# A softmax transpose moved off TensorE: 32x32 block transposes on VectorE and SBUF-to-SBUF DMAs

## The reference

```python
def chunked_rel_attention(q, k, v, rel_bias):      # 8 heads of width 64, 512 tokens
    ...
    scores = jnp.einsum("bnqhd,bnkhd->bnhqk", qc, kb) * (dh ** -0.5)
    bias = rel_bias[:, jnp.clip(dist, -REL_CLIP, REL_CLIP) + REL_CLIP]
    scores = jnp.where(valid, scores + bias[None, None], NEG_INF)
    p = jax.nn.softmax(scores, axis=-1)
    out = jnp.einsum("bnhqk,bnkhd->bnqhd", p, vb)

def hybrid_layer(x, ...):
    hn = rms_norm_2(x, norm_gain)
    proj = hn @ w_in                               # 4096 columns
    ...                                            # ya: attention, yr: retention, 4 heads of 128
    y = jnp.concatenate([ya * silu(ag), yr * silu(rg)], axis=-1)
    return x + y @ w_out
```

## Time and profile before

| | us |
|---|---|
| time, median of 3 runs (1222.36 to 1224.81) | 1222.63 |
| the profiled execution | 1224.13 |
| its span, first to last instruction | 1222.3 |
| PE busy | 1208.9 (99%) |
| PEld busy | 1027.0 (84%) |
| DVE busy | 842.9 (69%) |
| ACT busy | 589.4 (48%) |
| POOL busy | 287.8 (24%) |

### The profile page before, as it was taken

How to read it: one execution, slowest core, us unless ns; L and a number is a source line. 1 busy time by engine, 2 the same in 40 slices (tenths; PEclk the granted TensorE clock), 3 DMA queues, 4 the chain that set the end, 5 groups by cost and what they waited for, 6 DMA issues and landing times.

```text
span 1222.3 us, 15898 instructions
## 1 busy us (share of the span) xinstructions
PE 1208.9 (99%) x6061; PEld 1027.0 (84%) x6061; DVE 842.9 (69%) x1361; ACT 589.4 (48%) x1080; POOL 287.8 (24%) x299
## 2 busy tenths in 40 slices
PE   8999999999999999999999999999999999999998
PEld 7788888888888888888888879899888889899886
DVE  5889655556776577537758887767747686766746
ACT  6666432333433334224336477664435577654442
POOL 0220499912000000000006761111414211212300
PEclk8999999999999999999999999999999999999999
DMA  7422333233423433233324332222214332222211
GB/s 218 124 83 64 101 87 103 88 102 95 130 78 90 126 96 94 86 108 100 103 70 131 90 99 88 79 85 71 69 52 138 109 91 87 78 69 71 77 45 69
DMA packets 196032, 114.35 MB, mean 94 GB/s; under 512 B 3994, under 2 KB 190836, under 8 KB 195828
## 3 DMA queue, kind: packets, MB, share of 16 engines
q1 hardware_dynamic: 195956, 113.35, 31.5%
HBM read 111.23 MB, written 2.10 MB: 93 GB/s over the span
## 4 chain that ended last, share of the span: by engine, by line
PE 95%; DVE 3%; ACT 1%; issue 1%; DMA 1%; SPq 0%; DVEq 0%; ACTq 0%
PE ps L190 92%; PE ps L193 3%; DVE b_sets L163 1%; DMA xtm<-in_x_dram 1%; DVE wlo L163 0%; ACT b_p L160 0%; ACT whi L160 0%; DVE fold L163 0%; ACT x1l L160 0%; DVE b_pt L163 0%; DVE tmp L163 0%; DVE b_s L166 0%; SPq L196 0%; DVE nrm L166 0%; DVE b_sets L166 0%
## 5 line engine op out<-in xcount | busy, mean ns | idle before, releaser
L160 ACT ACTIVATE whi<-raw 128x1024 fp32r<-128x1024 f32 (+1 forms) x198 | 206.6, 1051 | 294.1 <-PE ps L190 293.7
L163 DVE TENSOR_TENSOR wlo<-raw,whi 128x1024 fp32r<-128x1024 f32 (+1 forms) x192 | 245.4, 1285 | 50.5 <-ACT whi L160 49.8
L190 PE MATMUL ps<-x0l,whi 128*128 128x512 f32 x1008 | 257.6, 394 | 0.0
L190 PE MATMUL ps<-x0h,whi 128*128 128x512 f32 x1008 | 255.4, 391 | 0.0
L190 PE MATMUL ps<-x0h,wlo 128*128 128x512 f32 x1008 | 254.3, 390 | 0.0
L190 PEld LDWEIGHTS ps<-x0h,whi 128*128 128x128 f32 x1008 | 188.0, 188 | 38.1
L190 PEld LDWEIGHTS ps<-x0h,wlo 128*128 128x128 f32 x1008 | 187.8, 188 | 38.3
L190 PEld LDWEIGHTS ps<-x0l,whi 128*128 128x128 f32 x1008 | 186.5, 188 | 37.4
L163 POOL TENSOR_TENSOR sums<-sums,sq 128x512 f32<-128x512 f32 x28 | 43.2, 1555 | 423.6 <-ACT sq L160 423.6
L190 PE MATMUL ps<-x1h,wlo 128*128 128x512 f32 x304 | 82.3, 389 | 0.0
L190 PE MATMUL ps<-x1h,whi 128*128 128x512 f32 x304 | 82.3, 389 | 0.0
(11 more groups left out here) (187 smaller groups left out, 1705.6 us busy)
## 6 DMA issues: line engine op xcount, KB each, us to landing
raw<-in_w_in_dram SPq DMA_DIRECT2D x98, 512.0 KB, 4.0
raw<-in_w_up_dram SPq DMA_DIRECT2D x44, 512.0 KB, 3.8
raw<-in_w_out_dram SPq DMA_DIRECT2D x24, 512.0 KB, 3.6
raw<-in_w_down_dram SPq DMA_DIRECT2D x16, 512.0 KB, 3.6
b_m<-in_rel_bias_dram SPq DMA_DIRECT2D x16, 256.0 KB, 3.3
raw<-in_w_down_dram SPq DMA_DIRECT2D x8, 384.0 KB, 3.1
xtm<-in_x_dram SPq DMA_DIRECT2D x4, 512.0 KB, 7.5
raw<-in_w_attn_branch_dram SPq DMA_DIRECT2D x8, 256.0 KB, 2.9
```

Of the source, the lines that this page charges most:

```text
L160: return AC.put(lambda e: e.activation(o, i, func, **kw), after, AC, 1)
L163: return on.put(lambda e: e.tensor_tensor(o, a, b, op), after, on, 1)
L190: return PE.put(lambda e: e.matmul(o, l, r, start=start, stop=stop), after, PE if mark else None, 1)
```

## The change

The ten PE transposes of a head are gone. At R, DVE turns the same weights in 32x32 blocks (six `STREAM_TRANSPOSE` instructions, 1280 columns in all) into `PD`, and sixteen DMAs, each of 32 partitions and 320 columns (40 KB), carry every block row from `PD` to its place in `PX`. At R+3 ACT makes the high half of all 1280 columns in one instruction, at R+4 DVE the low half in one; the eight value matmuls stay at R+6 and read in a new order of columns (runs of 32 to 128 columns, four of them), which the last DVE addition sets right. To make room, the raw weight ring goes from 5 to 3 buffers, the second bias buffer moves into the low half of `X1`'s slot 4 (so its first DMA waits for the last matmul of the stage ahead, and slot 4 for the last reader of the bias), and the mask becomes a tile and a DMA of its own. The six `FOLD` instructions move from the start to just before `rotary_turns`.

```diff
-        NRAW, NW = 5, 4
+        NRAW, NW = 3, 4
...
-        SETS, PB, PTB, S2, MB = pool_plan("b_", [
+        SETS, PB, PTB, S2, MB, PD, PX = pool_plan("b_", [
...
+            ("s2", 1024, F32), ("m", 512, F32), ("pd", 1280, F32), ("px", 1280, F32)])
+        MB2 = at("mb2", 512, x1_off + 4 * (4096 + 4 * 512))
...
-        t_c = dma(CA[:, 128:451], const_a[:, 128:451], d_c)
+        dma(MASKN, const_a[:, 128:384], d_c)
+        t_c = dma(CA[:, 128:195], const_a[:, 384:451], d_c)
...
         def spread_a():
             rb["rb"] = spread_rows(RB[:, :], va["diag"], 7)
-            t = tt(FOLD[:, 0:32], IDENT[:, 0:32], IDENT[:, 32:64], ALU.add, after=rb["rb"])
-            ...
+        t = tt(FOLD[:, 0:32], IDENT[:, 0:32], IDENT[:, 32:64], ALU.add, after=rb["rb"])
+        ...
 
         rotary_turns()
...
+            ms.free[1] = [ms.free[1], W.done[W.n_take - 1]]
             load_bias(0)
             load_bias(1)
...
                 ms.free[km] = [tm[1]]
+                if km == 1:
+                    slot_free[4].append(tm[1])
...
-                t0 = turn(0, 5, 0, claim(5))
-                free = claim(6)
-                turn(1, 6, 0, free)
-                t1 = turn(3, 6, 384, free)
-                yield 1
+                pd = PD[:, :].rearrange("p (i x c) -> p x i c", i=4, c=32)
+                for t, k0, k1, x0, x1, dx in ((0, 0, 1, 0, 1, 1), (1, 0, 2, 1, 5, 3), (2, 0, 2, 2, 6, 3), (2, 2, 3, 7, 8, 1),
+                                              (3, 0, 2, 3, 7, 3), (3, 2, 4, 8, 10, 1)):
+                    tb = blocks(pd[:, x0:x1:dx, :, :], p[t][:, 128 * k0:128 * k1].rearrange("p (k i c) -> p k i c", i=4, c=32),
+                                after=[t_p[t], pd_free[0]])
+                pbs.free[kp] = [tb]
+                for j in range(4):
+                    for d in range(4):
+                        t_px = dma(PX[32 * d:32 * d + 32, 320 * j:320 * j + 320], PD[32 * j:32 * j + 32, 320 * d:320 * d + 320],
+                                   d_px, after=[tb, px_free[0]])
+                pd_free[0] = [t_px]
+                yield 3
                 _, pt, tfree = ptbs.take()
                 hi, lo = pt[:, 0:1280], pt[:, 1280:2560]
-                ...
+                th = act(hi, PX[:, :], after=[t_px, tfree])
+                yield 1
+                tl = tt(lo, PX[:, :], f32(hi), ALU.subtract, after=[t_px, th, tfree])
+                px_free[0] = [th, tl]
+                yield 2
                 o, free = PS[7], claim(7)
+                by_q = lambda a, x0, x1: a.rearrange("p (q x) -> p q x", q=4)[:, :, 32 * x0:32 * x1]
                 for kt in range(4):
-                    n = 512 - 128 * kt
                     vk = v_at(s // 2, kt)[:, s % 2, 128 * e:128 * e + 128]
-                    mm(o[:, 128 * kt:512], vk, hi[:, PT_K[kt]:PT_K[kt] + n], kt == 0, False, after=[tok_v[s // 2], th, free])
-                    tp = mm(o[:, 128 * kt:512], vk, lo[:, PT_K[kt]:PT_K[kt] + n], False, kt == 3, after=tl, mark=kt == 3)
+                    x0, x1 = AT_K[kt], AT_K[kt] + 4 - kt
+                    mm(by_q(o[:, :], kt, 4), vk, by_q(hi, x0, x1), kt == 0, False, after=[tok_v[s // 2], th, free])
+                    tp = mm(by_q(o[:, :], kt, 4), vk, by_q(lo, x0, x1), False, kt == 3, after=tl, mark=kt == 3)
...
-                t2 = tt(backwards(YB[r, :]), tiles(o[r, :]), tiles(t[r, :]), ALU.add, after=[t1, yfree])
+                q4 = lambda a: a.rearrange("p (q t c) -> p q t c", q=4, t=4)
+                y = YB[r, :].rearrange("p (t q c) -> p q t c", q=4, t=4)[:, ::-1, :, ::-1]
+                t2 = tt(y, q4(o[r, :]), q4(t[r, :]), ALU.add, after=[t1, yfree])
```

More of the change, by code:

```diff
@@ L140, in block_then_hybrid_layers @@
         IDENT = CA[:, 0:128]
[L141 to L145, removed]
+        MASKN = MASK[:, :]
+        INVF = CA[:, 128:129]
+        SGN = CA[:, 129:130]
+        TWOPI = CA[:, 130:131]
+        AHEAD = CA[:, 131:195]
         TURN = [part * 2.0 ** (-12 * i - 12) for i, part in enumerate((0x28B, 0xE60, 0xDB9, 0x391, 0x054))]
@@ L848, in spread_a @@
             rb["rb"] = spread_rows(RB[:, :], va["diag"], 7)
-            t = tt(FOLD[:, 0:32], IDENT[:, 0:32], IDENT[:, 32:64], ALU.add, after=rb["rb"])
-            for i in (64, 96):
-                t = tt(FOLD[:, 0:32], FOLD[:, 0:32], IDENT[:, i:i + 32], ALU.add, after=t)
-            va["fold"] = [copy(FOLD[:, i:i + 32], FOLD[:, 0:32], after=t) for i in (32, 64, 96)]
         banks = Banks([3, 5, 1, 2, 0])
@@ L901, in rotary_sines @@
             rot["tok"] = [c, act(ROT[:, 512:1024], ROT[:, 512:1024], ACT.Sin, scale=SGN, after=rot["turns"])]
+        t = tt(FOLD[:, 0:32], IDENT[:, 0:32], IDENT[:, 32:64], ALU.add, after=rb["rb"])
+        for i in (64, 96):
+            t = tt(FOLD[:, 0:32], FOLD[:, 0:32], IDENT[:, i:i + 32], ALU.add, after=t)
+        va["fold"] = [copy(FOLD[:, i:i + 32], FOLD[:, 0:32], after=t) for i in (32, 64, 96)]
         rotary_turns()
@@ L1289, in head @@
+                pbs.free[kp] = [tb]
[5 more added lines that the diff above has]
+                yield 3
                 _, pt, tfree = ptbs.take()
                 hi, lo = pt[:, 0:1280], pt[:, 1280:2560]
-                th = [act(hi[:, 512 * j:512 * j + 512], PS[5 + j][:, :], after=[(t0, t1)[j], tfree]) for j in range(2)]
+                th = act(hi, PX[:, :], after=[t_px, tfree])
@@ L1292, in head @@
                 yield 1
-                tl = [tt(lo[:, 512 * j:512 * j + 512], PS[5 + j][:, :], f32(hi[:, 512 * j:512 * j + 512]),
-                         ALU.subtract, after=[th[j], tfree]) for j in range(2)]
-                bank_free[5], bank_free[6] = [tl[0]], [tl[1]]
-                yield 1
-                tp = turn(2, 5, 0, claim(5))
-                pbs.free[kp] = [tp]
-                yield 1
-                th.append(act(hi[:, 1024:1280], PS[5][:, 0:256], after=tp))
-                yield 1
```

17 lines of the change are left out of this document (8 added, 9 removed).

## The result

| | before | after |
|---|---|---|
| time, median us | 1222.64 (4 runs, 1222.36 to 1224.81) | 1283.78 (4 runs, 1282.55 to 1284.75) |
| span of the profiled execution | 1222.3 | 1281.9 |
| PE busy | 1208.9 | 1216.8 |
| PE idle within the span | 13.4 | 65.1 |
| mean granted clock | 0.996 | 0.974 |

The change makes the kernel slower: the ratio is 1.0496, 95% interval 1.0477 to 1.0514, or 61 us. I had forecast 1211.4 us, with a range from 1202 to 1223.

The account below looks back on a forecast made before the run. The prediction took PE, busy 1208.9 of 1222.3 us, as the bound, with DVE as second limit. Transposes -18.1, bank-5 wait -1.2, FOLD -0.9 and new waits +9.0 made -11.2 us: 1222.63 to 1211.4, range 1202 to 1223.

Parts of the forecast that it names:

- the price of an issue: SP's queue: each of a head's sixteen DMA issues takes 0.38 us, 6.1 us in all.
- The four waits of PE near the heads 2 and 6: PE waits for DVE's query halves in both layers: 3.9 + 3 x 1.7 = 9.0 us.
- rival 3: The DMA chain is the bound: value matmuls wait if an issue costs over 0.56 us; slower, 1250 us; chance 0.12.
- PE's transposes: Ten transposes a head leave PE: 1.13 us each head, 18.1 us over sixteen heads, at least 14.7.
- Bank-5 wait: PE's wait at 717.24 for DVE to free bank 5 for head 0's last transposes goes: 1.2 us.
- `FOLD`: Moving these DVE instructions from the start removes most of a 1.26 us PE wait at 40.64: 0.9 us.
- Value matmuls in runs: On PE, reading and writing in runs of 32 to 128 columns costs nothing; upper bound 23.5 us.
- rival 4: Strided value matmuls on PE cost double, 1234.9 us, or half of it; chance 0.06.
- DVE's transposes: Block transposes of 1280 columns add 1.8 us a head on DVE, bounds 1.4 and 4.2.
- DVE's low half even: One 1280-column instruction from SBUF takes up to 1.84 us, against 1.8 us before from PSUM.
- rival 2: DVE is the bound, with waits for it spread over all heads: -3.8 us, 1218.8 us; chance 0.14.
- Landing 1.9 us: The last of a head's sixteen DMAs lands after as long as a 64 KB load, 1.9 us.

Follow-up runs that it names:

- experiment 2: Changed kernel with eight or four DMAs a head for sixteen, same bytes, blocks not in place (time alone); 1212.24 and 1210.50 us.
- experiment 4: Changed kernel with four DMAs writing to HBM scratch and one reading back, for the sixteen; order of the change; 1236.29 us, ratio 1.0107.
- the version at 1205.5: Changed kernel with four HBM writes and one read, transposes one step earlier, ACT's half, DVE's half, value matmuls 5, 6, 7 steps behind; 1205.47 us.
- experiment 1: Changed kernel with the ten transposes of a head back on PE, the side edits (smaller rings, bias buffer, mask, FOLD) kept; 1222.87 us, ratio 0.9995.
- x_early_late: Changed kernel, sixteen DMAs kept, block transposes one step earlier, ACT's and DVE's halves two and one steps later; 1245.11 us, ratio 1.0178.

## Why the prediction was wrong

**The step that failed is the price of an issue**, "sixteen take 16 x 0.38 = 6.1 us". It was 0.63 us, 10.1 us a head. The chain came to 11.4 us instead of 8.0. I took the issue of a load that stood alone (0.34) for one in a row. The trace of before had the better row, on the SP queue, which I had passed over: every `w_conv_branch` tile is issued right behind a `w_attn_branch` tile, and costs more than one that is issued alone (duration ns min/median/max):

```profile
L196 SPq DMA_DIRECT2D raw<-in_w_attn_branch_dram x8: 368/368/368, 111.9 to 221.1; - x8
L196 SPq DMA_DIRECT2D raw<-in_w_conv_branch_dram x8: 508/508/509, 112.3 to 221.5; - x8
```

Standing in a row is not all of it: even the first issue of a head, with the queue idle before it, lasts 0.51 us from `PD` to `PX` (the 507 ns of the rows in experiment 2), and the ones behind it 0.59. The 0.70 us of the earlier trace rows was nearer, and I explained it away by four large loads. Even 16 x 0.51 + 1.9 would have made a chain of 10.1 us.

**The sum was wrong besides.** The round trip in the order of the change (experiment 4) has a chain of 8.3 us, about the 8.0 of the prediction, and takes 1236.3 us where 1211.4 were forecast. So 25 of the 72 us that the forecast missed lie in its other terms, and the price of an issue accounts for the other 47. These are the steps. ACT was to reach the high half 7 us behind R and stand there for 1 us, with nothing due behind it; it is there after 4.2 and stands for 4.06. The four waits of PE near the heads 2 and 6 are 16.5 us, not 9.0, and 7 us of smaller waits (the scores of tile 1, the values, one for `h`) come to them. And the clock, which no term had, makes the larger part of 10.9 us of longer busy time.

**A second error stood in rival 3.** It had the price and the direction right ("over 0.56 us", slower), but charged only the value matmuls: at 0.63 it gives 16p + 1.9 + 2.9 = 14.9 against 13.7, or 1.2 x 16 = 19 us, which would just eat the gain. By its own numbers the four waits at the heads 2 and 6 grow with the chain as well. A chain of 11.4 instead of 8.0 us adds 3.4 to each of 3.9, 1.7, 1.7 and 1.7, which is 22.6 in all; measured are 6.8, 7.4, 5.4 and 5.8, which is 25.4. So the path of these waits was right (DVE's list up to the query's half) and their size roughly, and rival 3 should have carried them. That the sum comes so near is in part luck, since at the round trip's chain the same working gives 10.2 and 16.5 were measured. With sixteen waits of ACT behind it this rival deserved far more than 0.12.

The other steps, one by one:

- **PE's transposes, -18.1 (at least 14.7):** right. PE busy goes from 1208.9 to 1191.3 in the version at 1205.5, which is -17.6.
- **Bank-5 wait -1.2 and `FOLD` -0.9:** the first is right, no transposes wait for `b_pt` at 717 any more. The `FOLD` wait of 1.26 us is down to 0.7, so it gave 0.6 instead of 0.9.
- **Value matmuls in runs, 0:** right, rival 4 falls. At 728.94 eight take 1.22 us to the next start, before 1.32 (from 724.87, by the start behind it).
- **DVE's transposes, 1.8 us a head:** right. The row at 707.51 has 1.80 us. By form after the change (busy us, mean ns), and last the row of the kernel before with the 698 ns that the prediction worked from, which the earlier trace rows does not show:

```profile
L182 DVE STREAM_TRANSPOSE b_pd<-b_p 128x256 f32<-128x256 f32 x64 | 24.1, 410 | 0.6
L182 DVE STREAM_TRANSPOSE b_pd<-b_p 128x128 f32<-128x128 f32 x32 | 9.2, 287 | 1.9 <-ACT b_p L161 1.9
...
L181 DVE STREAM_TRANSPOSE sq<-sums 128x512 f32<-128x512 f32 x2 | 1.4, 698 | 0.0
```

- **DVE's low half even:** 1.49 us instead of 1.8, a little better. DVE was never the bound (rival 2): in the version at 1205.5 it is busy for 76 of 90 us and PE for 90 of 90.
- **Landing 1.9 us:** right to the digit, and counted from the start of the last issue, so that sixteen at 0.38 would have made 7.6 us and not 8.0. That one small load from HBM gave the digit for copies within SBUF is luck: with 80 KB they took 2.1. The 2.0 us that the prediction takes from the Trainium skill, "DMA: Bandwidth & Descriptors", stand there in the section Anatomy of one DMA and for DMAs issued from POOL; here they were issued from SP.
- **Three raw buffers and the other edits, 0:** right by themselves (experiment 1), and with the sixteen DMAs in the queue ACT waits 2.6 us for raw tiles in the two layers.
- **"So the value matmuls do not wait":** wrong, 15.7 us (8.0 for ACT's half, 7.7 for DVE's), and the scores of tile 1 wait 8.9 us for DVE's bias, which stood behind ACT's and DVE's halves.
- **PE waits for no `whi` or `wlo`:** right; its last sign of being wrong did not show.
- **The clock was no term of the sum at all.** The same 5901 matmuls are busy for 1216.8 us here and 1191.3 in the version without long gaps, 25.5 us more. In the two layers there are eleven stretches with a granted clock of 0.50, 61.3 us in all, and PE is busy for 45.4 us of them. Half of that, 22.7 us, is an estimate of what the clock took. The rest is open: in `x_early_late`, where the mean clock is 0.995, PE is busy for 9.5 us more than in that version, so something besides the clock lengthens the busy time where the gaps are many and short.

The account of the span: PE idle 13.4 to 65.1 is +51.7; busy -17.6 for the removed work and +25.5 for slower matmuls behind gaps, mostly the clock. Together +59.6, the whole difference of the spans.

## What to carry to other kernels

Count DMA issues as instructions of their engine, at the price of one right behind another in the trace, and add the landing from the start of the last one: a chain of many small DMAs is long by its count, not its bytes, and a few larger ones through HBM can be shorter. Where engines play one list each, work that waits for a transfer belongs at the place in the list where the transfer is over; one instruction placed 7 us too early holds everything that PE wants next. And when a chain turns out longer than assumed, every wait in the estimate that hangs on it grows with it, and the clock falls on top. When a time comes out as forecast, compare the chain too: the eight DMAs gave the forecast's 1212 us with a chain of 6.6 us, and the round trip, whose chain was the forecast's, gave 1236.

## What the runs showed of the hardware

- An SP issue within SBUF in a row costs 0.63 us from start to start with 40 and 80 KB and 0.64 with 160 KB, and lasts 0.51 as the first of a row; a load from HBM issued alone lasts 0.34 to 0.37. From POOL it is 0.52 (4.14 for eight), from ACT 0.67 (5.38 for eight), beside SP's own at 0.63. Writes to HBM of 160 KB were issued faster: four in 1.91 us.
- From the start of the issue, 40 KB from SBUF to SBUF landed in 1.9 us, 80 KB in 2.1, 160 KB in 2.2. To HBM 160 KB took 2.7, and 640 KB back 4.0.
- A PE gap of 6.8 us was followed by 3.4 us at a granted clock of 0.56, and one of 2.87 us by 6 us at 0.51.
